# Attention over a paged cache: every fourth K page pair multiplied with the query by GpSimd, in place in its ring slot

## What is computed

```
def stick_breaking(q, k, v, bias, q_pos, k_pos):
    z = jnp.einsum('bqhd,bkhd->bhqk', q, k) * (HEAD_DIM ** -0.5) + bias
    mask = k_pos[None, :] < q_pos[:, None]
    log_keep = jnp.where(mask, jax.nn.log_sigmoid(-z), 0.0)
    later = lax.cumsum(log_keep, axis=3, reverse=True) - log_keep
    w = jnp.where(mask, jnp.exp(jax.nn.log_sigmoid(z) + later), 0.0)
    return jnp.einsum('bhqk,bkhd->bqhd', w, v)
```

## Time and profile before

| | |
|---|---|
| median of 3 runs | 3632.18 us (3630.4 to 3633.06) |
| profiled execution, its own time | 3639.77 us |
| its span | 3638.1 us |
| busy over the span | PE 92%, DVE 56%, ACT 39%, POOL 18% |
| attention stage, L1474 (DVE multiply of a K pair) | 256 times, 324.5 us |
| attention stage, L1479 (DVE reduction) | 256 times, 313.2 us |

### The profile page before, as it was taken

How to read it: one execution, slowest core, us unless ns; L and a number is a source line. 1 busy time by engine, 2 the same in 40 slices (tenths; PEclk the granted TensorE clock), 3 DMA queues, 4 the chain that set the end, 5 groups by cost and what they waited for, 6 DMA issues and landing times. The chain is left out here.

```text
span 3638.1 us, 48630 instructions
## 1 busy us (share of the span) xinstructions
PE 3346.9 (92%) x14901; PEld 2305.5 (63%) x14901; DVE 2042.9 (56%) x2832; ACT 1401.6 (39%) x2214; POOL 637.5 (18%) x725
## 2 busy tenths in 40 slices
PE   6999875699999999998699799999999999999998
PEld 5888652343444444343588587787778777877777
DVE  5110449799888988985445455425542555245542
ACT  4110110365665666563333344324432443223332
POOL 2000054354444443442011100000000000000000
PEclk8999977799999999998799899999999999999999
DMA  3211261579889888986445433433343334334333
GB/s 128 76 65 56 82 79 28 165 255 300 283 289 304 276 287 284 302 295 221 157 139 154 129 98 93 134 110 104 93 133 110 105 93 124 123 124 121 122 108 116
DMA packets 487628, 569.61 MB, mean 157 GB/s; under 512 B 64808, under 2 KB 308616, under 8 KB 485321
## 3 DMA queue, kind: packets, MB, share of 16 engines
q1 hardware_dynamic: 482950, 549.81, 49.0%
q10 hardware_dynamic: 4328, 17.05, 1.2%
q0 software_dynamic: 176, 0.56, 0.0%
HBM read 506.91 MB, written 59.30 MB: 156 GB/s over the span
## 5 line engine op out<-in xcount | busy, mean ns | idle before, releaser
L2273 PE MATMUL ffn_bank<-ffn_xh,ffn_wh 128*128 128x512 f32 x1408 | 557.8, 396 | 19.0 <-DVE ffn_wl L2487 18.6
L2273 PE MATMUL ffn_bank<-ffn_xl,ffn_wh 128*128 128x512 f32 x1408 | 549.4, 390 | 0.0
L2273 PE MATMUL ffn_bank<-ffn_xh,ffn_wl 128*128 128x512 f32 x1408 | 548.8, 390 | 0.0
L1291 POOL TENSOR_TENSOR att_S<-att_S,att_X 128x512 f32<-128x512 f32 (+3 forms) x256 | 345.5, 1349 | 291.9 <-PE att_bank L1574 231.9
L1474 DVE TENSOR_TENSOR att_prod<-att_Kr,att_q_wide 128x1024 f32<-128x1024 f32 x256 | 324.5, 1268 | 13.0 <-DMA att_Kr<-in_cache_k_dram 9.5
L1569 PE MATMUL att_bank<-att_X,att_negtri 128*128 128x512 f32 (+3 forms) x640 | 299.7, 550 | 30.7 <-DVE att_X L1445 30.2
L2273 PEld LDWEIGHTS ffn_bank<-ffn_xh,ffn_wh 128*128 128x128 f32 x1408 | 264.9, 188 | 95.1 <-DVE ffn_wl L2487 31.4
L1479 DVE TENSOR_REDUCE att_z_s<-att_prod 128x16 f32<-128x1024 f32 x256 | 313.2, 1223 | 8.8
L2273 PEld LDWEIGHTS ffn_bank<-ffn_xh,ffn_wl 128*128 128x128 f32 x1408 | 264.9, 188 | 56.3
L2273 PEld LDWEIGHTS ffn_bank<-ffn_xl,ffn_wh 128*128 128x128 f32 x1408 | 265.2, 188 | 52.6
L2491 DVE TENSOR_TENSOR ffn_wdl<-ffn_wdf,ffn_wdh 128x1024 fp32r<-128x1024 f32 x88 | 107.5, 1225 | 334.8 <-ACT ffn_wdh L2397 334.7
(11 more groups left out here) (378 smaller groups left out, 5930.3 us busy)
## 6 DMA issues: line engine op xcount, KB each, us to landing
att_Kr<-in_cache_k_dram SPq DMA_DIRECT2D x512, 256.0 KB, 3.8
att_Vr<-in_cache_v_dram SPq DMA_DIRECT2D x512, 256.0 KB, 3.8
ffn_wdf<-in_w_down_dram SPq DMA_DIRECT2D x108, 512.0 KB, 3.3
ffn_stage<-in_w_gate_dram SPq DMA_DIRECT2D x89, 512.0 KB, 3.9
ffn_stage<-in_w_up_dram SPq DMA_DIRECT2D x88, 512.0 KB, 4.5
qku_work<-in_x_prompt_dram SPq DMA_DIRECT2D x16, 512.0 KB
att_qf<-qT_dram SPq DMA_DIRECT2D x64, 128.0 KB, 3.7
att_kf<-kT_dram SPq DMA_DIRECT2D x64, 128.0 KB, 3.7
```

What stands on the lines that cost most here:

```text
L1291: pool.tensor_tensor(new[:, r:], old[:, r:], x[:, r:], ALU.add).then_inc(s_part, 1)
L2273: mm = pe.matmul(bank[:, first + f % 2, :], w[:, j, k, :], x[:, k, :], start=(k == 0 and n == 0), stop=(k == KD - 1 and n == 2))
```

## The change

Of the 32 K pairs of a sequence, kk = 3, 7, ..., 31 are no longer multiplied by DVE. GpSimd multiplies them, and writes the product over the page pair in its ring slot. DVE waits for it (`k_pooled`) and reduces from the slot. GpSimd does the product of pair u + 3 ahead of its sum of unit u, for u = 0, 4, ..., 28. ACT's copy of the next queries waits for `k_summed` in place of `k_used`.

```
+        PERIOD = 4
+        POOLED = NKK // PERIOD
+        pooled = lambda kk: kk % PERIOD == PERIOD - 1
...
+                def key_product(b, kk):
+                    slot = Kr[:, kk % KSLOTS]
+                    if kk < PERIOD:
+                        pool.wait_ge(q_copied, b + 1)
+                    pool.wait_ge(k_loaded[kk % KSLOTS], 16 * PP * (b * (NKK // KSLOTS) + kk // KSLOTS + 1))
+                    pool.tensor_tensor(slot, slot, q_wide[:, None, :].to_broadcast([P, PP, AW]), ALU.mult).then_inc(k_pooled, 1)
+
                 def sums_round(b):
                     for u in range(NU):
+                        if u + 3 < NKK and pooled(u + 3):
+                            key_product(b, u + 3)
                         o, x = cols(u), X[:, u % NX, :]
...
-                    act.wait_ge(k_used, b * NKK)
+                    act.wait_ge(k_summed, b * NKK)
...
-                            tt(pr, Kr[:, kk % KSLOTS], q_wide[:, None, :].to_broadcast([P, PP, AW]), ALU.mult
-                               ).then_inc(k_used, 1)
-                            dve.wait_ge(k_used, b * NKK + kk + 1)
+                            if pooled(kk):
+                                dve.wait_ge(k_pooled, b * POOLED + kk // PERIOD + 1)
+                                pr = Kr[:, kk % KSLOTS]
+                            else:
+                                tt(pr, Kr[:, kk % KSLOTS], q_wide[:, None, :].to_broadcast([P, PP, AW]), ALU.mult
+                                   ).then_inc(k_used, 1)
+                                dve.wait_ge(k_used, b * (NKK - POOLED) + kk + 1 - (kk + 1) // PERIOD)
...
-                                              prod[:, kk % 2, :].rearrange("p (k h d) -> p k h d", k=PP, h=H), AX.X, ALU.add
+                                              pr.rearrange("p k (h d) -> p k h d", h=H), AX.X, ALU.add
```

More of the change, by code:

```diff
@@ L1123, in stage_attention @@
         k_loaded, v_loaded = m.sems("k_loaded", KSLOTS), m.sems("v_loaded", VSLOTS)
-        k_used, k_summed, v_used = m.sem("k_used"), m.sem("k_summed"), m.sem("v_used")
+        k_used, k_pooled, k_summed, v_used = m.sem("k_used"), m.sem("k_pooled"), m.sem("k_summed"), m.sem("v_used")
         zb_s, x_s_ready, e_s, l_s, sp_s, r_s, sum_s, logw_s, w_s_ready = (
```

## The result

| | kernel before | changed kernel |
|---|---|---|
| median of 7 runs, us | 3632.18 (3629.44 to 3634.64) | 3646.61 (3642.41 to 3654.88) |
| ratio, 95% interval | | 1.0043 (1.0032 to 1.0055) |
| profiled execution: own time / span, us | 3639.77 / 3638.1 | 3648.96 / 3647.3 |

The kernel got 14 to 16 us slower. The forecast was 3638 with a range of 3631 to 3654: the side and the range held, the size was 8.6 us short. The two profiled executions are only 9.2 us apart, because the one of before lies 7.6 above its median and the one of after 2.4. At 3639.77 us the profiled execution of before is slower than each of the 81 timed ones on record (the slowest took 3638.5), so differences of a few tenths of a microsecond a round against it are not safe.

A forecast was written before the change was run, and what follows sets the result against it. Round 0 was taken as DVE bound, looped rounds as held by SP's issue of K loads. Round 0 +2.7, round 1's start +1.8, looped rounds 0, round 7 -0.7 and +2 left out gave about +6: 3638 us, range 3631 to 3654.

The forecast's parts named there:

- The product, 2.37 us: One 128 x 1024 multiply on GpSimd, estimated from its sums at 2.37 us, bounds 2.0 and 3.1.
- A product holds a multiply to 0.14 us before its end: GpSimd's product holds DVE's multiply until 0.14 us before the product ends, up to 2.2 us.
- Round 0, DVE bound, +2.7: Round 0: each of 8 products loses 1.58 us by a hold and wins 1.25, +2.7 us in the round.
- The start of a looped round, +1.8: Product 3 goes first, so DVE's first multiply waits 1.8 us and k_summed of pair 0 comes 1.8 later.
- Late in a looped round: GpSimd waits for pairs 27 and 31; PE loses 2.7 us at its sums, and the att_own wait shrinks to 0.5.
- The looped rounds come out even: 0: Looped rounds: period 127.1 us against 127.3 before, counted as no change.
- SP's pace stands in the way of less: Looped rounds: SP issues K loads at its own pace, about 127 us a round, so they get no shorter.
- Round 7, -0.7: Round 7, with no wait for K pages, adds 1.1 us in place of 1.8, so -0.7.
- +2 for the products of pairs 7 to 23: A further 2 us for holds by these products, where DVE is ahead of PE, left out of the hand count.
- Added waits: Rival: PE falls idle in steps 5, 28 and 32 and the clock drops behind it; +16, 3648 us, chance 0.27.
- Dear product: Rival: a GpSimd product takes 3.1 us, 0.7 longer; +20 in all, 3652 us, chance 0.07.
- Faster and nothing: Two rivals: multiplies hardly held (0.4 us), 3624 us, chance 0.07; nothing shows, SP's pace swallows it, 3632, chance 0.04.

The follow-up runs named there:

- experiment 2: Changed kernel, but GpSimd writes zeros twice over the page pair in place of the product, behind the same waits: 3627.1 us, ratio 0.9992.
- no product: Changed kernel, but GpSimd does no products and DVE does not wait for them; pairs 3, 7, ..., 31 are multiplied by nobody: 3620.3 us, ratio 0.9966.
- only 3: Changed kernel, but only pair 3 of each round is multiplied by GpSimd: 3642.8 us, ratio 1.0040; run again 3642.5 us, ratio 1.0032.
- only 7 to 23: Changed kernel, but only pairs 7, 11, 15, 19 and 23 are multiplied by GpSimd: 3633.4 us, ratio 1.0012.
- only 27 and 31: Changed kernel, but only pairs 27 and 31 of each round are multiplied by GpSimd: 3636.1 us, ratio 1.0011.

## Why the prediction came out as it did

- **The product, 2.37 us:** the median is 2.362. Right.
- **A product holds a multiply to 0.14 us before its end:** 0.11 at the round's start, multiplies of up to 3.19 us, and with a product that only writes, the hold is gone. Right, shown by experiment 2.
- **Round 0, DVE bound, +2.7:** +1.9. Right, and for the reason given: the 9.7 us that round 0 wins with no product are used up by holds. In the timelines of GpSimd and DVE in round 0 of the changed kernel the product comes first, as the prediction had read it from the earlier trace rows:
```profile
730.84 2.36 POOL L1286 TENSOR_TENSOR att_Kr<-att_Kr,att_q_wide 128x1024 f32<-128x1024 f32 x1
731.50 2.78 DVE L1490 TENSOR_TENSOR att_prod<-att_Kr,att_q_wide 128x1024 f32<-128x1024 f32 x1
```
The multiply is held 1.56 us; the prediction said 1.58.
- **The start of a looped round, +1.8:** +1.66 in each of rounds 1 to 6. Right.
- **Late in a looped round:** GpSimd stands at pairs 27 and 31, PE waits for sums in steps 28 and 32, 1.0 and 1.2 us (forecast 1.5, and 2.7 in all; with what the start and pairs 7 and 23 add, PE is 4.3 late after step 33). The wait for `att_own` falls to 1.66 and not to 0.5: a late sum holds DVE's 0.68 us instruction for 0.8, and DVE waits 0.81 for ACT's copy, both in front of `att_own`. Right in kind, 0.3 us too early in `att_own`.
- **"The looped rounds come out even: 0":** wrong. With the hold at the start of round 1, which the prediction counted apart, +1.8 was forecast for rounds 1 to 6 and +9.9 measured. This is the step that failed, by one round that was taken for all. Round 3 was the longest: its period was 128.97 and its way to `att_own` 104.0, where the mean way was 102.35 + 0.74 = 103.1 (0.74 from DVE's start to PE's). Its first K load came 1.78 us behind `k_summed(0)`, the mean was 0.93. So the prediction let SP take up 1.6 us of the late start, and a mean round had only 0.7 to give. The mean period of 127.3 was set beside round 3's way, so the rest of the round came out as 23.3; a mean round's was 127.3 - 103.1 = 24.2. With the mean for both the prediction's own steps give 103.7 + 24.2 - 1.7 + 1.8 = 128.0, or +0.7 a round and +4 in six. (With round 3 for both they give 103.7 + 24.97 - 1.7 + 1.8 = 128.8 against 128.97, even again, so it is the choice of the round that counts.) The period was 128.97; the remaining 1.0 is 0.3 at `att_own`, and the clock's echo: c fell by 0.93 and not by 1.7, and by the clock's means (0.9524 after, 0.9520 and 0.9527 before) it may have gained nothing.
- **SP's pace stands in the way of less:** the other way round. SP's slack, 0.93 us in the mean with 0.19 left after, was used up by the late start. With only 3 it absorbed up to half of the delay (b is 0.6 to 0.85 shorter), and in the changed kernel none of this shows in b, where GpSimd's late products put `att_own` off.
- **Round 7, -0.7:** from step 0 to the last `att_own` 159.24 in place of 159.78, -0.5. Right in size, wrong in its way: here DVE's first multiply came first (1586.39, 1.21 us) and held the product (3.89 us), which then held the second multiply (1.97).
- **+2 for the products of pairs 7 to 23:** only 7 to 23 cost +4 by the medians. Of the right order.
- **Sum:** against the profiled execution 3645.6 was forecast and 3649.0 measured, 3.4 short. The other 5 us of the 8.6 are how far each profiled execution lay from its own median, which no step could know. That is luck of the draw, and it went against the forecast; in the other direction it would have hidden the error in the looped rounds.
- **The rivals.** Added waits (3648) has the nearest number, and its mechanism is seen in part. The clock fell to 0.50 in new places: behind step 5 in rounds 3 and 6 (rows above) and once in step 32, in round 1. The kernel before has it in looped rounds in steps 34 and 35 alone. But it is not "once per looped round on top": over the six rounds the clock stands at 0.50 for 24 us against 27 before, and the 10 us of that rival would have lowered the mean clock by 0.003 (10 us lost is 20 us at 0.50, in 3640), where it is 0.9524 against 0.9520 to 0.9527. What was added is the start's 1.66 and 0.93 on the way to `att_own`. Dear product: the product is not dear. Faster and nothing: excluded by the interval. Without the hold the change would have been nothing to slightly faster (experiment 2: -3), so the faster rival named the right condition.

Not settled: why only 27 and 31 costs +4 by the medians when neither its round 0 (116.8) nor its looped rounds (126.93) are longer than before in the profiled execution. That one execution of before accounts for about 4 us of this by the estimate above, half of the gap; a single execution differs from the next by as much. What the best use of the idea would be was not looked for beyond this: no set of pairs that was run is faster than the kernel before.

## What to carry to other kernels

Before work is taken off VectorE and given to GpSimd, look whether both read two operands from SBUF at the same time, and add up the holds before the relief (here 64 x 1.25 = 80 us off, of which 61 were lost again to the products' holds). Ask where in a period a delay falls, since 1.7 us at the start cost 7 us a kernel and the same in the middle nothing. And read a slack from all rounds: one round had 1.8 us of it, the mean had 0.9. An effect of a few tenths a round can't be read from one execution that lies 7.6 us above its median; here the mean clock of all executions said more.

## What was not expected

Piece c of a round, `att_own` to step 0, takes mostly one of three lengths in every kernel: 17.1, 18.8 or 20.4 us, 1.65 apart (before: 18.80, 18.78, 20.05, 18.83, 18.78, 20.41; only 27 and 31: 18.78, 18.78, 17.14, 17.13, 17.12, 17.13). In the windows that is the granted clock, 0.50 for a stretch, for two, or for none. Equal waits don't give equal lengths: in the changed kernel all waits for `att_own` in rounds 2 to 6 are 1.65 or 1.66 us, and the clock behind them differs. Windows just behind the wait in round 3 (c is 17.13) and in round 5 (18.76), changed kernel:
```profile
1179.00:1183.00 4.00, 3.96 (x18) 2.15 (x18) 3.94 (x12) 3.92 (x8) 1.20 (x2) 1.00 0.92 315
1436.00:1440.00 4.00, 4.00 (x13) 1.71 (x12) 3.90 (x13) 3.92 (x8) 0.40 (x1) 0.71 0.91 308
1440.00:1444.00 4.00, 4.00 (x14) 1.79 (x14) 1.94 (x5) 1.59 (x4) 1.28 (x1) 0.86 0.94 324
```
In this kernel a saved or added microsecond of TensorE's waiting for `att_own` is worth nothing, or 1.6 us, or 3.3, and a mean over rounds is needed to price it.
